# Experts with 32 places in four column tiles, and two more places for their weights

## The reference

```
p_group = softmax(t @ w_rg + b_rg); group = top 1 of 4 groups
e_logits = (t @ w_re + b_re) of that group's 8 experts; top 2 of them
combine[token, expert] = w_top of the two, normalised, times p_top
a = t @ w_gate[e];  u = t @ w_up[e]        # 1024 -> 512, 32 experts
out += (silu(a) * u * combine[:, e]) @ w_down[e]   # 512 -> 1024
```

## Time and profile before

| | |
|---|---|
| median of 3 runs | 2601.15 us (2600.13 to 2604.54) |
| the profiled execution | 2596.7 us, span 2594.8 us, granted clock 0.981 |
| TensorE, matmuls | 2450.3 us busy (94% of the span) |
| VectorE, ScalarE, GpSimd | 858.7, 537.8 and 57.8 us busy |
| moved by DMA | 653.77 MB, mean 252 GB/s |
| share of TensorE in the chain that ended last | 87% |

### The profile page before, as it was taken

How to read it: one execution, slowest core, us unless ns; L and a number is a source line. 1 busy time by engine, 2 the same in 40 slices (tenths; PEclk the granted TensorE clock), 3 DMA queues, 4 the chain that set the end, 5 groups by cost and what they waited for, 6 DMA issues and landing times.

```text
span 2594.8 us, 28240 instructions
## 1 busy us (share of the span) xinstructions
PE 2450.3 (94%) x11508; PEld 1601.2 (62%) x11508; DVE 858.7 (33%) x2061; ACT 537.8 (21%) x1168; POOL 57.8 (2%) x86
## 2 busy tenths in 40 slices
PE   8999999999999999999989999999899989999997
PEld 7888678847865885568754444444677644444443
DVE  4754456421252754334431111111534421111112
ACT  4332311001351100214421111111315211111111
POOL 0000000000100000002000000000020000000000
PEclk9999999999999999999989999999899999999999
DMA  7222246675713677443349999999542279999995
GB/s 277 91 74 97 98 162 238 242 281 138 239 65 137 244 277 274 156 162 98 130 168 415 397 414 417 419 418 408 178 158 102 112 311 392 415 411 415 397 414 235
DMA packets 141885, 653.77 MB, mean 252 GB/s; under 512 B 7386, under 2 KB 13834, under 8 KB 117040
## 3 DMA queue, kind: packets, MB, share of 16 engines
q1 hardware_dynamic: 138336, 642.46, 63.2%
q0 software_dynamic: 3408, 9.38, 1.6%
HBM read 648.66 MB, written 3.15 MB: 251 GB/s over the span
## 4 chain that ended last, share of the span: by engine, by line
PE 87%; DVE 6%; issue 3%; ACT 2%; DMA 2%; DVEq 0%; ACTq 0%
PE ps L106 84%; PE ps L109 2%; DMA bias_rows<-AR 2%; DVE AR L125 1%; ACT AR L115 1%; DVE AR L129 1%; ACT L115 1%; DVE AR L120 1%; DVE AR L133 0%; DVE X L125 0%; DVE XN L133 0%; DVE XN L121 0%; ACT wring L115 0%; DVE XN L125 0%; ACT SM L115 0%
## 5 line engine op out<-in xcount | busy, mean ns | idle before, releaser
L106 PE MATMUL ps<-wring,AR 128*64 128x512 f32 (+3 forms) x3776 | 927.0, 584 | 56.3 <-issue 47.8
L106 PEld LDWEIGHTS ps<-wring,AR 128*64 128x64 f32 (+2 forms) x3776 | 370.7, 145 | 578.9 <-issue 574.0
L106 PE MATMUL ps<-HT,wring 128*128 128x256 f32 x3200 | 721.8, 387 | 0.8 <-ACT wring L115 0.4
L106 PEld LDWEIGHTS ps<-HT,wring 128*128 128x128 f32 x3200 | 617.0, 194 | 92.8 <-issue 4.2
L115 ACT ACTIVATE AR<-ps 128x512 f32<-128x512 f32 (+6 forms) x274 | 137.9, 503 | 966.9 <-PE ps L106 535.0
L125 DVE TENSOR_TENSOR AR<-ps,AR 128x512 f32<-128x512 f32 (+2 forms) x116 | 66.5, 573 | 639.7 <-PE ps L106 635.4
L106 PE MATMUL ps<-AR 128*128 128x128 f32 (+5 forms) x1304 | 263.2, 364 | 5.3 <-DVE AR L141 2.4
L106 PEld LDWEIGHTS ps<-AR 128*128 128x128 f32 (+2 forms) x1304 | 169.3, 189 | 95.0 <-issue 80.7
L129 DVE SCALAR_TENSOR_TENSOR wring<-wring,CC 128x512 f32<-128x512 f32 x168 | 126.3, 752 | 6.0
L106 PE MATMUL ps<-AR,XN 128*128 128x128 f32 x1024 | 123.9, 280 | 1.9 <-DVE AR L137 1.9
L106 PEld LDWEIGHTS ps<-AR,XN 128*128 128x128 f32 x1024 | 120.8, 197 | 2.5 <-issue 2.1
(11 more groups left out here) (150 smaller groups left out, 1333.7 us busy)
## 6 DMA issues: line engine op xcount, KB each, us to landing
wring<-in_w_gate SPq DMA_DIRECT2D x64, 2048.0 KB, 13.6
wring<-in_w_up SPq DMA_DIRECT2D x64, 2048.0 KB, 9.2
wring<-in_w_down SPq DMA_DIRECT2D x64, 2048.0 KB, 12.3
wring<-in_w_ada SPq DMA_DIRECT2D x24, 2048.0 KB, 11.8
wring<-in_ffn_w_up SPq DMA_DIRECT2D x20, 2048.0 KB, 8.8
wring<-in_w_in SPq DMA_DIRECT2D x18, 2048.0 KB, 7.6
wring<-in_w_out SPq DMA_DIRECT2D x10, 2048.0 KB, 8.8
wring<-in_ffn_w_down SPq DMA_DIRECT2D x10, 2048.0 KB, 13.0
```

Source lines behind the costliest of these rows:

```text
L106: return Ins(self.eng and self.eng.matmul(out, lhs, rhs, start=start, stop=stop), None)
```

## The change

The number of places an expert has (`CAP`) goes from 64 to 32; the test for the other branch goes with it. The 64 rows of a pair become 32 + 32, and the array is used as four tiles of 32 columns:

- In `up`, each expert has two tiles, one for each half of the input features (blocks 0 to 3 and 4 to 7). Gate and up now leave in PSUM two half sums an expert, on different rows.
- `inner` turns and adds them in one: each 128x128 block is the stationary side against a matrix `fold` of 64 columns, eight matmuls instead of four transposes. SiLU and the product come after it, and gate and up are copied out of PSUM plain before it.
- In `lower`, the four tiles are two halves of the output columns by two experts; the output is one bank instead of two, and VectorE alone copies it. ScalarE no longer does.
- `scatter` works with 64 rows at a time, upper or lower by the half of the output; `weigh` writes the weighted selection twice for that.
- The tiles of the experts become smaller and move below 8224 in the arena, or into MN. The two freed pieces of 4096 columns at the end of the arena become two more slots of `W`, from the first up weights of a layer (after the last attention output has been computed) to the layer's last down weights (`widen`, `narrow`).
- The final gains go into `MG` instead of `MF`, and `id2` is taken out of the constants.

```diff
-CAP = 64
+CAP = 32
...
+    def widen(self, name, *events):
+
+        extra = list(range(len(self.places) - self.spare, len(self.places)))
+        self.order = extra + self.order
+        for i in extra:
+            self.held[i] = name
+        self.free(name, *events)
+
+    def narrow(self):
+        self.order = [i for i in self.order if i < len(self.places) - self.spare]
...
-    parts["id2"] = np.stack([(p[:, None] + 128 * k == t[None]) for k in range(2)], 1).reshape(128, 512)
+    parts["fold"] = (p[:, None] // 64 == np.arange(64)[None] // 32) & (p[:, None] % 32 == np.arange(64)[None] % 32)
...
-    slots = [dma(f"w{i}") for i in range(NSLOT)]
-    W = Ring([wring[:, i * SLOT:(i + 1) * SLOT] for i in range(NSLOT)])
+    slots = [dma(f"w{i}") for i in range(NSLOT + 2)]
+    W = Ring([wring[:, i * SLOT:(i + 1) * SLOT] for i in range(NSLOT)] + [AR[:, ARENA - i * SLOT:ARENA - (i - 1) * SLOT] for i in (2, 1)], 2)
...
+                    if p == 0 and name == "eup":
+                        W.widen(("arena", layer), (sig(f"att_mm{layer}"), ("o", 3)))
                     for x in range(2):
                         expert((name, layer, 2 * p + x), src[layer, 2 * p + x], kt, n)
+            W.narrow()
...
-                        ins = e.matmul(ps[:, j * 128:j * 128 + 128], XN[:, m, k * 128:k * 128 + 128], sel[:, m, :], m == 0, m == 1)
+                        ins = e.matmul(ps[:, j * 64:j * 64 + 64], XN[:, m, k * 128:k * 128 + 128], sel[:, m, :], m == 0, m == 1)
...
             def up(p):
...
-                    for k in range(8):
+                    for k in range(4):
                         for x in range(2):
-                            ins = e.matmul(ps[64 * x:64 * x + 64, :], hg[:, k, 64 * x:64 * x + 64], wx[x][:, k, :], k == 0, k == 7)
+                            for h in range(2):
+                                r = 64 * x + 32 * h
+                                ins = e.matmul(ps[r:r + 32, :], hg[:, 4 * h + k, 32 * x:32 * x + 32], wx[x][:, 4 * h + k, :], k == 0, k == 3)
...
             def inner(p):
+
                 ps = bank(e, PB, ("t", p))
-                e.wait_ge(vect, ("act", p))
-                for f in range(4):
-                    ins = e.transpose(ps[:, f * 128:f * 128 + 128], AC[p][:, f, :], IDENT)
+                for n, (tile, ready) in enumerate(((GC[p], (act, ("gate", p))), (UC[p], (vect, ("eup", p))))):
+                    e.wait_ge(*ready)
+                    for f in range(4):
+                        c = 256 * n + 64 * f
+                        ins = e.matmul(ps[:, c:c + 64], tile[:, f, :], C("fold", 64), True, True)
                 ins.then_inc(done, ("t", p))
 
             def lower(p):
                 wd = [weights(("edown", layer, 2 * p + x), 4, 1024) for x in range(2)]
-                y = [bank(e, PB, ("y", p, c)) for c in range(2)]
-                e.wait_ge(act, ("t", p))
+                y = bank(e, PB, ("y", p))
+                e.wait_ge(vect, ("act", p))
                 for f in range(4):
                     for c in range(2):
                         for x in range(2):
-                            ins = e.matmul(y[c][64 * x:64 * x + 64, :], AT[p][:, f, 64 * x:64 * x + 64],
-                                           wd[x][:, f, c * 512:c * 512 + 512], f == 0, f == 3)
+                            r = 64 * c + 32 * x
+                            ins = e.matmul(y[r:r + 32, :], AT[p][:, f, 32 * x:32 * x + 32], wd[x][:, f, c * 512:c * 512 + 512], f == 0, f == 3)
...
             def scatter(p):
...
-                e.wait_ge(*((sig(f"join_a{layer}"), "end") if p == 15 else (act, ("y", p))))
                 for m in range(2):
                     for c in range(2):
-                        ins = e.matmul(PA[("moe", layer), m, c][:, :], SWT[p][:, tok(m)], YS[p][:, c * 512:c * 512 + 512], p == 0, p == 15)
+                        r = slice(64 * c, 64 * c + 64)
+                        ins = e.matmul(PA[("moe", layer), m, c][:, :], SWT[p][r, tok(m)], YS[p][r, :], p == 0, p == 15)
...
             for p in range(16):
-                ac = AC[p]
+                uc = bank(v, UC, p)
                 v.wait_ge(read, ("eup", p))
-                v.wait_ge(act, ("silu", p))
-                v.tensor_tensor(ac, turned_order(PB["eup", p][:, :]), ac, MUL).then_inc(done, ("act", p))
-                PB.free(("eup", p), (done, ("act", p)))
+                v.tensor_copy(uc, turned_order(PB["eup", p][:, :])).then_inc(done, ("eup", p))
+                PB.free(("eup", p), (done, ("eup", p)))
+                UC.free(p, (mm, ("t", p)))
                 if p < 15:
                     select(layer, p + 1)
                     weigh(layer, p + 1)
+                at_ = AT[p]
+                v.wait_ge(*((sig(f"join_a{layer}"), "end") if p == 15 else (act, ("silu", p))))
+                v.tensor_tensor(at_, four(PB["t", p][:, 256:512]), at_, MUL).then_inc(done, ("act", p))
+                PB.free(("t", p), (done, ("act", p)))
+                if p < 15:
                     collect(layer, p + 1)
                 ys = bank(v, YS, p)
                 v.wait_ge(read, ("edown", p))
                 key = (sig(f"join_v{layer}"), "end") if p == 15 else (done, ("y", p))
-                v.tensor_copy(ys[:, 512:1024], PB["y", p, 1][:, :]).then_inc(*key)
-                PB.free(("y", p, 1), key)
+                v.tensor_copy(ys, PB["y", p][:, :]).then_inc(*key)
...
-                empty(bank(a, AC, p), turned_order(PB["gate", p][:, :]), (read, ("gate", p)), done, ("silu", p), ACT.Silu)
+                empty(bank(a, GC, p), turned_order(PB["gate", p][:, :]), (read, ("gate", p)), done, ("gate", p))
...
-                empty(bank(a, AT, p), four(PB["t", p][:, :]), (mm, ("t", p)), done, ("t", p))
-                PB.free(("t", p), (done, ("t", p)))
+                key = (sig(f"join_a{layer}"), "end") if p == 15 else (done, ("silu", p))
+                empty(bank(a, AT, p), four(PB["t", p][:, 0:256]), (mm, ("t", p)), *key, ACT.Silu)
```

More of the change, by code:

```diff
@@ L160, with __init__ @@
 class Ring:
-    def __init__(self, places):
-        self.places, self.freed, self.where, self.before = places, {}, {}, {}
+    def __init__(self, places, spare=0):
+        self.places, self.freed, self.where, self.before, self.spare = places, {}, {}, {}, spare
         self.restart()
     def restart(self):
-        self.order, self.held = list(range(len(self.places))), [None] * len(self.places)
+        self.order, self.held = list(range(len(self.places) - self.spare)), [None] * len(self.places)
+    def widen(self, name, *events):
[6 more added lines that the diff above has]
+        self.order = [i for i in self.order if i < len(self.places) - self.spare]
     def defer(self):
@@ L397, in build @@
     QT = at(8192, 5, 256)
-    LGT, CB, MK, RK, FL = at(6144, 2, 40), at(6224, 2, 32), at(6288, 2, 32), at(6352, 2, 32), at(6416, 2)
+    LGT, CB, MK, RK, FL = at(4096, 2, 40), at(4176, 2, 32), at(4240, 2, 32), at(4304, 2, 32), at(4368, 2)
     FLAG = FL[0:1, 1:2].bitcast(I32)
@@ L438, in moe_rings @@
     def moe_rings(layer):
[L439 to L445, removed]
+        return (ring(("sel", layer), lambda: [(at(4372 + 384 * j, 2, 64), at(4500 + 384 * j, 2, 128)) for j in range(2)]),
+                ring(("hg", layer), lambda: [MF[:, 512 * j:512 * j + 512].rearrange("p (k s) -> p k s", k=8) for j in range(2)]),
+                ring(("swt", layer), lambda: [at(5140 + 256 * j, 256) for j in range(2)]),
+                ring(("gc", layer), lambda: [at(5652, 4, 128)]),
+                ring(("uc", layer), lambda: [at(6164, 4, 128)]),
+                ring(("at", layer), lambda: [at(6676 + 256 * j, 4, 64) for j in range(2)]),
+                ring(("ys", layer), lambda: [MF[:, 1024 + 512 * j:1536 + 512 * j] for j in range(2)]))
     def dense_rings(layer):
-        n = 6418
+        n = 4372
         return (ring(("ga", layer), lambda: [at(n + 1024 * j, 4, 256) for j in range(2)]),
@@ L1342, in sparse @@
             PB = path_rings("sparse", layer)
-            SEL, HG, SWT, AC, AT, YS = moe_rings(layer)
+            _, HG, SWT, GC, UC, AT, YS = moe_rings(layer)
             def up(p):
@@ L1412, in dense @@
                     ps = bank(e, PB, ("cr", ex))
-                    for k in range(2):
-                        ins = e.matmul(ps[:, 0:256], bc(CB[:, k, ex:ex + 1], 128), C("id2", 512)[:, k * 256:k * 256 + 256], k == 0, k == 1)
+                    for m in range(2):
+                        ins = e.matmul(ps[:, tok(m)], bc(CB[:, m, ex:ex + 1], 128), IDENT, True, True)
                     ins.then_inc(done, ("cr", ex))
@@ L1881, in last_part @@
                 h = slice(512 * c, 512 * c + 512)
-                v.scalar_tensor_tensor(X[:, m, h], X[:, m, h], r, MF[:, h], MUL, MUL).then_inc(sig("last_v"), (tag, m, c))
+                v.scalar_tensor_tensor(X[:, m, h], X[:, m, h], r, (MG if tag == "final" else MF)[:, h], MUL, MUL).then_inc(sig("last_v"), (tag, m, c))
         def nsa():
@@ L2198, in collect @@
```

(30 more changed lines are left out.)

21 lines of the change are left out of this document (10 added, 11 removed).

## The result

The changed kernel took 2537.96 us (median of 4 runs, 2533.61 to 2538.4), the kernel before 2602.26 in the runs beside it: a ratio of 0.9749 [0.9732, 0.9766], 64.3 us less. Between the two profiled executions it is 2596.7 to 2537.92, 58.8 us less, where the prediction's sum said 71.4. The forecast of 2530 was 8 us too low.

The account below looks back on a forecast made before the run. Weight bytes at 428 GB/s were the floor, with losses from TensorE and DMA coupling. Stages of 452.4 us save 71.4 in all, taking 2596.7 to 2525.3; with 4.5 for spread, the forecast is 2530, range 2516 to 2566.

Parts of the forecast that it names:

- Two limits close together, lost in the coupling: Expert stages before: TensorE some 29 us a pair, DMA 29.4; late slot reads leave the queue short, giving 416 GB/s.
- Matmuls of 3.55: Gate, up and down bursts: four column tiles side by side take 3.55 us each instead of 7.09.
- Pair 18.6: All TensorE work for a pair of experts at full clock: 18.6 us, against 29.4 of DMA.
- Seven pieces ahead, 89 remain: Seven weight pieces are issued before each expert stage, two in new places, leaving 89 of 96 to load.
- T + 442.4 for the last landing: Last weights land 442.4 us after the first expert matmul T: 3.6 first issue, 2.7 latency, 436.1 for 89 pieces.
- Tail 10: Stage's end behind the last weights: 10 us taken, between 6.3 at full clock and 16.6 at half clock.
- Sum: Both expert stages become 452.4 us, saving 33.7 in layer 0 and 37.7 in layer 1, together 71.4.
- Bursts at half clock: Rival: every expert matmul burst starts at half clock, tails grow 6.6 us each, 2543; chance 0.14.
- Bytes at 416: Rival: expert weights still flow at 416 GB/s, 12.5 us more a layer, 2555, or 2568 with long tails; chance 0.17.
- Four tiles give nothing: Rival: four column tiles bring no speed, TensorE stays at 29 us a pair plus 1.3, about 2597; chance 0.04.
- Clock stays at 1.2 GHz: Rival: TensorE's clock stays low throughout the expert stages, 33.8 us a pair, about 2707; chance 0.04.
- full-width branch: Rival: an expert has over 32 tokens, so the other branch's wide matmuls run, about 3490; chance 0.03.

Follow-up runs that it names:

- e10: Changed kernel with five weight places instead of seven and gate, up and down matmuls each done twice: 2603.06 us, 1.003 of the kernel before.
- e9: Changed kernel, seven weight places kept, with gate, up and down matmuls each done twice: 2558.16 us, 0.9851 of the kernel before.
- e1: Changed kernel with the two extra weight places never opened, so five throughout: 2558.77 us, 0.9843 of the kernel before.
- a0: The changed kernel itself run again, unaltered, in a later set: 2538.52 us, 0.9775 of the kernel before.
- e6: Changed kernel loading only half of each weight piece, matmuls using that half twice, full-width branch ruled out: 2199.76 us in one execution.
- e5: Changed kernel with the two extra places opened only after the first pair's pieces were all asked for: 2559.3 us, 0.9847 of the kernel before.
- e7: Changed kernel with an eighth weight place, in an arena made longer: 2527.59 us, 0.9731 of the kernel before.
- e4: Changed kernel with each layer's first gather streaming 128 columns again instead of 64: 2531.06 us, 0.9741 of the kernel before.
- e8: Changed kernel with an eighth weight place and each layer's first gather over 128 columns: 2521.77 us, 0.9712 of the kernel before.
- e2: Changed kernel with matmul loops reordered, meant to let only two column tiles work at a time; seven places: 2546.16 us, 0.9798 of the kernel before.

## Why the prediction came out as it did

The mechanism was right and the forecast near; the sum behind it was 12.7 us too large, in three terms that stand below. The four corners show the mechanism (time, stages):

| | five places | seven places |
|---|---|---|
| matmuls slow | 2603 (e10; 489.4, 484.3) | 2558 (e9; 464.8, 465.6) |
| matmuls fast | 2559 (e1; 467.8, 466.9) | 2538 (a0; 457.8, 456.7) |

They come from three sets of runs on three chips, in which the kernel before took 2596.3 to 2597.1. The two causes do not add: the first of either is worth some 44 us, the second 20. Either takes away the coupling. What the second adds under the bound of bytes is, for two places, two pieces a layer; for fast matmuls, an earlier first issue (in layer 0 T + 6.6 in a0 for T + 8.4 in e9, with T the first expert matmul) and a shorter tail (8.2 for 12.1).

Step by step:

- *Two limits close together, lost in the coupling*: right. 416 became 427 (e1) and 426 (e9), and neither fast matmuls nor more places was needed for the other to do it. That each would do alone was not said.
- *Matmuls of 3.55*: 3.62 to 3.64 at full clock. *Scatter 2.0*: 1.99. *Gather 3.7*: 3.74. *Inner 1.9*: 2.00. *Pair 18.6*: 18.08 in e6, as neighbouring bursts overlap a little. Right.
- *Seven pieces ahead, 89 remain*: right, and each counts once: e5 (none), e7 (5.5 a layer for one).
- *T + 442.4 for the last landing*: here the sum failed. In layer 0 it was T + 449.4 (1766.6 + 21.7 = 1788.3). 3.0 of the 7.0 are the gate slots, free at T + 6.6 instead of T + 3.6, because the burst ran near half clock; I had taken the size of full clock for the one burst that sets the first issue, although the gather ahead of it stands in the earlier trace rows at 5.79, where the later one takes 3.74. e4 shows the term: with a gate burst of 3.64 the last landing is T + 446.8. The other 4.0 are the rate: 449.4 - 6.6 - 2.7 leaves 440.1 for 89 pieces, 4.94 each instead of 4.90. Over 425 us in the middle it is 428 GB/s, so they lie mostly at the ends. The next layer's `w_in`, asked for from 1766.95 on, shares the queue there, but it is not all: in layer 1 no load follows, and the last landing is T + 448.8, with 3.4 of the same kind. There DMA moves 285 GB/s over 2069 to 2074 and 214 over 2505 to 2511; by these rates, as an estimate, start and end cost 4.7 us where the sum had 2.7. What remains was not traced.
- *The start of the stage*: taken as unchanged. The first gather of a layer stands in front of T, and it took 1.3 longer; from its start to T it is 8.7 us for 7.7 in both layers (1330.22 to 1338.90, 2053.73 to 2062.42; before 1330.21 to 1337.89, 2081.15 to 2088.83). That is the +1.0 in front of layer 0 and 1.0 of the +2.6 between the stages. The other 1.7 are the scatter of layer 0, whose saving comes to nothing, as the next point shows.
- *Tail 10*: 6.7 in layer 0 and 8.7 in layer 1; I had chosen between 6.3 and 16.6 and taken too much. In layer 0 down stood at full clock behind the up burst, in layer 1 its middle was at half. It gives back 3.3 and 1.3. (In the 16.6, inner stands at 1.9, its size at full clock.) In layer 0 the scatter's shortening by 1.7 is worth nothing besides, though the stage's length counts it: VectorE goes on 5.2 us after its last copy whatever the scatter takes, and from the start of the scatter to the next transposes it is 1793.02 to 1803.50, 10.5 us. In the timeline of the kernel before, where the scatter begins at 1820.30, it is 10.5 as well:

```profile
1825.52 0.69 DVE L125 TENSOR_TENSOR XN<-ps,AR 128x512 f32<-128x512 f32 x1 [5.27 <-issue]
...
1830.81 1.51 PE L109 MATMUL ps<-CS,XN 128*128 128x128 f32 x6 [6.80 <-DVE XN L121]
```

- *Sum*: 33.7 + 37.7 predicted, 30.0 + 32.6 - 3.9 outside them measured, so 12.7 less: 3.7 in layer 0 (7.0 - 3.3), 5.1 in layer 1 (6.4 - 1.3) and 3.9 outside. That 2530 missed by 8.0 only is in part luck: I had added 4.5 us for the spread of the kernel before, and the profiled execution of the kernel after lies at its median (2537.92, 2537.96). The rest to the medians is spread too: the profiled execution of before was 5.6 below the median beside it.

The rivals. *Bursts at half clock* (2543) holds for a part of them: the up bursts, after up to 6.2 us of idle, take mostly 5.0 to 6.6, gate and down mostly 3.64. Inside the stage that costs nothing, since DMA holds 428 over it. In the tail of layer 1 it cost 1.7, as the down burst took 5.34 for 3.64. The Trainium skill ("TensorE: Matmul & The Clock Gate", HAM oscillation) has bursts behind DMA waits start cold, and only a part agrees. The up burst at 1778.56, after 6.16 us of idle, is slow from its first records (1.07 us for a pair of them, 0.62 at full clock). The one at 1364.29, after 2.71 us, starts at full pace and slows 0.9 us in, and so does the one of 8.78 in the earlier trace rows, with a granted clock of 1.00 over 1405 to 1406 and 0.51 over 1406 to 1409; the prediction counted that one as agreeing. *Bytes at 416* falls by the windows. *Four tiles give nothing* falls by 3.64 and e6. *Clock stays at 1.2 GHz* falls except for the first gather and burst, where it is 0.51. The full-width branch was not taken.

## What to carry to other kernels

When a stage is close to two limits, find what couples them (here: a slot is free only once it has been read) before adding up gains; two changes that each remove the coupling do not add. Where the bytes bind and the matmuls are fast enough (e5), a place in the ring is worth just the piece it lets you load before the stage starts, and the time from the stage's start to its first freed slot counts in full, as does the tail behind the last byte. Cost these two ends at the clock that they will have, not at that of the middle.

## What the runs showed of the hardware that was not expected

- Behind a narrower gather the clock stayed low longer. A gather of 32 records with 64 moving columns took 7.06 us and the gate burst behind it 6.51; with 128 columns it was 5.87 and 3.64 (e4), in both cases after the same sparse stretch of small matmuls. Granted was 0.51 over 1335 to 1345 in the kernel after. In all runs the six first gathers with 128 columns (the kernel before, e4, e8) took 5.4 to 6.2, the twenty with 64 columns 7.06 each. That this width alone makes the difference is shown by e4 and e8, in both layers; why is not.
- Matmuls for free column tiles begin while earlier ones in the program's order still wait for theirs (e2: 5.4 us for two tiles after two, not 7.1).
- The 428 GB/s of the earlier trace rows held for over 400 us (426 to 428 in the runs without dips). That fits what the Trainium skill says of a core alone ("Perfetto Trace Analysis", Roofline: about 435 GB/s over 16 DMA engines, more than its share of 358, which it has when both cores of a pair draw on the memory). The prediction took the 358 for a core's limit.
